# The next turn's rows turned later in the first expert turn, and the gate copies moved behind the first rows

## What is computed

```python
def swiglu(x, w_gate, w_up, w_down):
    return (jax.nn.silu(x @ w_gate) * (x @ w_up)) @ w_down

def moe_ffn(x, w_router, e_gate, e_up, e_down):
    logits = jnp.einsum('btd,de->bte', x, w_router, preferred_element_type=jnp.float32)
    top_v, top_i = lax.top_k(logits, TOP_K)
    w = jax.nn.softmax(top_v, axis=-1)
    gates = jnp.sum(jax.nn.one_hot(top_i, N_EXPERTS, dtype=jnp.float32) * w[..., None], axis=-2)
    out = jnp.zeros(x.shape, jnp.float32)
    for e in range(N_EXPERTS):
        out = out + gates[..., e:e + 1] * swiglu(x, e_gate[e], e_up[e], e_down[e]).astype(jnp.float32)
    return out.astype(x.dtype)
```

## Time and profile before

| | us |
|---|---|
| median of 3 runs (lowest, highest) | 1843.89 (1839.78, 1846.74) |
| the profiled execution | 1837.21 |
| its span, first to last instruction | 1835.4 |
| TensorE busy | 1629.8 |
| VectorE busy | 775.1 |
| ScalarE busy | 630.0 |
| GpSimd busy | 426.8 |

### The profile page before, as it was taken

How to read it: one execution, slowest core, us unless ns; L and a number is a source line. 1 busy time by engine, 2 the same in 40 slices (tenths; PEclk the granted TensorE clock), 3 DMA queues, 4 the chain that set the end, 5 groups by cost and what they waited for, 6 DMA issues and landing times.

```text
span 1835.4 us, 25783 instructions
## 1 busy us (share of the span) xinstructions
PE 1629.8 (89%) x10579; PEld 1447.5 (79%) x10580; DVE 775.1 (42%) x1073; ACT 630.0 (34%) x781; POOL 426.8 (23%) x209
## 2 busy tenths in 40 slices
PE   5999998979999999999699998988578998998991
PEld 2898667869999999998598766877577987897891
DVE  1204666351222222222512566533757545744742
ACT  3410443343111111112521244224356344644631
POOL 1430004344333333333442002430511010110003
PEclk9999999989999999999799998996689999998996
DMA  8220673214122211111031253101578564875834
GB/s 341 104 73 31 230 253 130 77 47 150 69 85 78 88 69 69 69 69 69 23 130 49 88 194 144 69 23 58 204 242 309 212 227 164 299 239 174 297 116 139
DMA packets 42285, 252.44 MB, mean 138 GB/s; under 512 B 5024, under 2 KB 7200, under 8 KB 15936
## 3 DMA queue, kind: packets, MB, share of 16 engines
q1 hardware_dynamic: 35200, 226.67, 34.2%
q0 software_dynamic: 6256, 21.56, 4.4%
q10 hardware_dynamic: 720, 2.62, 0.4%
HBM read 231.43 MB, written 19.46 MB: 137 GB/s over the span
## 4 chain that ended last, share of the span: by engine, by line
PE 74%; DVE 10%; DMA 5%; ACT 5%; issue 3%; POOL 3%; SPq 0%; POOLq 0%; DVEq 0%; ACTq 0%
PE ps L376 26%; PE ps L768 11%; PE ps L674 8%; PE ps L781 5%; PE ps L641 5%; DMA raw<-stream 4%; PE ps L481 3%; PE ps L502 2%; PE ps L586 2%; DVE wl L1807 2%; DVE smn L1528 2%; DVE probs L1544 2%; ACT wh L1359 2%; PE ps L513 1%; PE ps L572 1%
## 5 line engine op out<-in xcount | busy, mean ns | idle before, releaser
L993 POOL TENSOR_TENSOR wl<-raw,wh 128x2048 fp32r<-128x2048 f32 x61 | 286.7, 4709 | 743.6 <-ACT wh L1156 743.4
L768 PE MATMUL ps<-wh,xg 128*128 128x256 f32 x1536 | 295.4, 290 | 21.6 <-issue 15.9
L1807 DVE TENSOR_TENSOR wl<-raw,wh 128x2048 fp32r<-128x2048 f32 x96 | 219.9, 2292 | 136.9 <-ACT wh L1359 133.4
L768 PEld LDWEIGHTS ps<-wh,xg 128*128 128x128 f32 x1536 | 250.3, 198 | 24.9 <-issue 21.6
L376 PE MATMUL ps<-hn_h,wh 128*128 128x320 f32 x1088 | 252.2, 313 | 13.4 <-ACTq L1341 8.4
L376 PE MATMUL ps<-hn_l,wh 128*128 128x320 f32 x1088 | 249.2, 310 | 0.0
L376 PE MATMUL ps<-hn_h,wl 128*128 128x320 f32 x1088 | 249.1, 310 | 0.0
L1359 ACT CAST wh<-raw 128x2048 fp32r<-128x2048 f32 x96 | 183.1, 1909 | 124.8 <-PE ps L768 48.9
L768 PE MATMUL ps<-wl,xg 128*128 128x256 f32 x768 | 221.5, 288 | 0.0
L376 PEld LDWEIGHTS ps<-hn_h,wh 128*128 128x128 f32 x1088 | 182.6, 189 | 18.2 <-ACTq L1341 11.0
L376 PEld LDWEIGHTS ps<-hn_h,wl 128*128 128x128 f32 x1088 | 183.2, 189 | 0.0
(11 more groups left out here) (243 smaller groups left out, 2671.3 us busy)
## 6 DMA issues: line engine op xcount, KB each, us to landing
raw<-stream SPq DMA_DIRECT2D x205, 1024.0 KB, 4.8
sum_d<-zero POOLq DMA_DIRECT2D x7, 512.0 KB, 6.1
x<-x SPq DMA_DIRECT2D x5, 512.0 KB, 9.8
hn_d<-hrow ACTq DMA_DIRECT2D x5, 512.0 KB, 2.6
eacc<-sum_d SPq DMA_DIRECT2D x5, 512.0 KB, 5.9
y<-x SPq DMA_DIRECT2D x5, 512.0 KB, 2.6
hn_d<-zero POOLq DMA_DIRECT2D x2, 512.0 KB, 11.7
consts<-consts SPq DMA_DIRECT2D x1, 968.5 KB, 4.8
```

What stands on the lines that cost most here:

```text
L768: last = mm(bank(b, st * COLS, (st + 1) * COLS), xg[h][:, k, part, st * 128:(st + 1) * 128], w[:, k * COLS:(k + 1) * COLS], start=(k == 0 ...
L993: nc.gpsimd.tensor_tensor(wl[s][:, :], raw[s][:, :], wh[s][:, :].bitcast(F32), ALU.subtract).then_inc(wl_ready, 1)
L1807: v.tensor_tensor(wl[s][:, :], raw[s][:, :], wh[s][:, :].bitcast(F32), ALU.subtract).then_inc(wl_ready, 1)
```

## The change

In the first turn alone (`first_turn`: p + h == 0) TensorE turns tile 0 of the next turn's rows behind gate 3 in place of gate 2, with its wait for the gather, into bank 1; and tiles 1, 2 and 3 behind down 2, into banks 3, 1 and 3. ScalarE and VectorE take the tiles up in the order that answers to it. Ahead of the first turn VectorE copies the gate rows behind the first rows' low parts and subtraction 2. No operation is added or taken away.

```diff
--- before.py
+++ after.py
@@ -344,6 +344,9 @@
         slot_ready = sem("slot_ready")
         ADDED_0 = 16 * (NT + 2)
 
+        def first_turn(p, h):
+            return isinstance(p, int) and p + h == 0
+
         def named(p):
             return p if isinstance(p, int) else "more"
 
@@ -793,14 +796,20 @@
                                     pe.nop().then_inc(bank_full[6 + hf], 1)
                         if (kind, q) in (("gate", 1), ("gate", 2), ("gate", 3)):
                             turn_hidden(p, h, q - 1, tiles)
-                        if more and (kind, q) == ("gate", 2):
+
+                        late = first_turn(p, h)
+                        if more and (kind, q) == ("gate", 3 if late else 2):
                             pe.wait_ge(rows_here[1 - h], 32 + h * 32 + p * 32)
-                            turn_rows((named(p), h), 1 - h, 0, 3)
-                        if more and (kind, q) == ("gate", 3):
+                            turn_rows((named(p), h), 1 - h, 0, 1 if late else 3)
+                        if more and not late and (kind, q) == ("gate", 3):
                             turn_rows((named(p), h), 1 - h, 1, 1)
                         if (kind, q) == ("down", EXP_BLK - 2):
                             turn_hidden(p, h, EXP_BLK - 1, tiles)
-                            if more:
+                            if more and late:
+                                turn_rows((named(p), h), 1 - h, 1, 3)
+                                turn_rows((named(p), h), 1 - h, 2, 1)
+                                turn_rows((named(p), h), 1 - h, 3, 3)
+                            elif more:
                                 turn_rows((named(p), h), 1 - h, 2, 3)
                                 turn_rows((named(p), h), 1 - h, 3, 1)
 
@@ -1407,10 +1416,12 @@
                     if q < EXP_BLK - 1:
                         turned_by(act, (named(p), h, "exp", "gate", q + 1), p)
                         exp_split((5, 8, 11)[q], p, h)
-                    if q and nxt:
-                        rows_high((named(p), h), 1 - h, q - 1, p)
-                if nxt:
-                    rows_high((named(p), h), 1 - h, 3, p)
+                    late = int(first_turn(p, h))
+                    if q > late and nxt:
+                        rows_high((named(p), h), 1 - h, q - 1 - late, p)
+                for j in range(3 - late, 4):
+                    if nxt:
+                        rows_high((named(p), h), 1 - h, j, p)
                 if more:
                     exp_split(N_EU + 1, p, h)
                 if isinstance(p, int) and p + h == 0:
@@ -1835,7 +1846,8 @@
                 low(7, p, h)
                 hidden_low(1)
                 low(8, p, h)
-                if nxt:
+                late = int(first_turn(p, h))
+                if nxt and not late:
                     rows_low((named(p), h), 1 - h, 0, p)
                 product(2)
                 low(9, p, h)
@@ -1843,15 +1855,14 @@
                 hidden_low(2)
                 low(11, p, h)
                 if nxt:
-                    rows_low((named(p), h), 1 - h, 1, p)
+                    rows_low((named(p), h), 1 - h, 1 - late, p)
                 product(3)
                 if more:
                     low(N_EU, p, h)
                 hidden_low(3)
-                if nxt:
-                    rows_low((named(p), h), 1 - h, 2, p)
-                if nxt:
-                    rows_low((named(p), h), 1 - h, 3, p)
+                for j in range(2 - late, 4):
+                    if nxt:
+                        rows_low((named(p), h), 1 - h, j, p)
                 if more:
                     low(N_EU + 1, p, h)
                     low(N_EU + 2, p, h)
@@ -1861,10 +1872,10 @@
                 places()
                 low(0)
                 low(1)
-                gate_rows(3)
                 for j in range(4):
                     rows_low("ahead", 0, j)
                 low(2)
+                gate_rows(3)
                 for e in range(E):
                     expert_turn(e // 2, e % 2, e < E - 1, e < E - 1)
                 dve.wait_ge(trips_ready, 1)
```

## The result

The changed kernel takes 1837.13 us (median of 20 runs, 1831.12 to 1841.31), the kernel before 1843.15, measured beside it (median of 20). One of the 20 executions of before took 3240.27 us and is left out of the ratio; without it the median is 1842.68. The ratio is 0.997, 95% interval 0.9961 to 0.9979: 5.5 us faster, between 3.9 and 7.2. The profiled execution has a span of 1834.3 us.

A forecast was written before the change was run, and what follows sets the result against it. TensorE's work (89% busy) plus its holes was taken as the bound, here the 12.82 us wait for gathered rows. 8.6 gained less 2.4 for later rows gives 6.2 us: 1837.7 from the median 1843.89, range 1831.5 to 1844.5.

The forecast's parts named there:

- Three units ahead of the wait; the hole shrinks: TensorE, first turn: up, down and gate units run before the row wait; idle shrinks from 12.8 to 3.7 us.
- W: When the next turn's gathered rows land and TensorE's wait for them ends; 1337.03 in the profile before.
- The drag: GpSimd list writes meeting running VectorE weight subtractions wait for their end; the last write ends 3.2 us later.
- W moves by 1.0 or 3.7, 2.4 taken: Rows land later by 1.0 or 3.7 us, as the first gather slips through or is caught; middle 2.4.
- W + 17.8 to the next turn: First turn's work from W to the next turn's start takes 17.8 us against 26.41, a gain of 8.6.
- the wait for tile 3's bank: Tiles 1 and 3 share a bank: TensorE waits 0.84 for VectorE's subtraction, then 0.9 for transposes, until W + 11.5.
- the lower bound with the fast down: Last down of the first turn takes 2.75 in place of 4.49 us: W + 16.1, gain 10.3.
- Part 2: Gate copies behind the first rows: first product 2.9 us earlier, copies covered, worth nothing by themselves ahead of a wait.
- All behind moves as a whole: Everything behind the first turn is tied to it and moves as a whole; 6.2 us gained.
- No drag: Rival: GpSimd's chain keeps its times, W stays 1337.0, gain 8.6 to 10.3, 1834.5 us; chance 0.27.
- Eaten in the next turn: Rival: the next turn's weight waits lengthen, leaving a gain of 0 to 3, 1842.5 us; chance 0.17.
- The late landing: Rival: gathered rows land late beside three more weight units, W 1348.1, 2.4 us slower, 1846.3; chance 0.08.

The follow-up runs named there:

- The fillers: Kernel before plus, in idle VectorE time, a two-SBUF-input subtraction (last list write ends +22.49) or, in another kernel, a one-input reduction (+19.43); one execution each.
- e2: Kernel before with only the gate copies moved behind the first rows' low parts and third weight subtraction; 1843.28 us, ratio to before 1.0.
- e1: Changed kernel with the gate copies back at their old place, so only the next turn's rows are turned late; 1837.28 us, ratio to before 0.9965.
- e4: Kernel before with the first three weight subtractions moved into VectorE's idle time ahead of the list writes; 1835.0 us, ratio to before 0.9951.
- e7: Changed kernel with tile 3 turned behind the last down in place of ahead of it; ratio to before 0.9975.
- e3: Changed kernel with the first three weight subtractions moved into VectorE's idle time ahead of the list writes; 1834.3 us, ratio to before 0.9955.
- e9: Kernel before with tile 0 alone turned behind the second down unit in place of the third gate, first turn; 1835.93 us, ratio to before 0.9962.

## Why the prediction came out as it did

The forecast was 1837.7 and 6.2 us of gain; measured are 1837.13 and 5.5, or 6.0 by the medians with the 3240.27 in. The number is closer than the steps are, which partly cancelled. By its steps:

- *Three units ahead of the wait; the hole shrinks.* Right. The hole went to 7.64 us, which with the later W and the earlier start was the expected 5 to 9.
- *The drag.* Right, in mechanism and size: the last write at +22.88 against a forecast +22.63, with just the four writes caught that were named (five, eight, nine, ten). The fillers and the row subtractions leave the second SBUF input as the cause. The first gather slipped through, which had been too near to call. One reading was wrong: not seven but six of the ten writes of before were free (four took 1.88 to 3.06); it stood on the side of the rival.
- *W moves by 1.0 or 3.7, 2.4 taken.* By the profile 1.96, made up of 0.4 more than the forecast end of the second gather's writing and a landing 0.6 slower (6.85). As a term of the kernel's time the 2.4 is not shown: e2 costs nothing (1.0, 0.9989 to 1.001), and e1 against the changed kernel shows no gain that the intervals can tell from none. In W it shows only weakly. The four kernels whose writes end at 19.4 have W of 38.4 to 41.7, the four at 22.4 to 22.9 have 39.7 to 43.7, so the drag is real on GpSimd and W's own scatter is as large.
- *W + 17.8 to the next turn.* Measured 16.9, but not by the forecast's terms. The last hidden low part ended at W + 10.3 (forecast 9.8), the wait for tile 3's bank came as forecast, and the last down started at W + 11.7 (forecast 11.5). From the hidden low part on the forecast added the bank wait, a down of 4.49 and a branch of 1.83, together 8.0 us; measured are 6.55, and 6.4 to 6.8 in every kernel. So neither the bank wait (1.7) nor the down's clock has a price of its own, and the lower bound with the fast down is no case: e4, with a fast down and no bank wait, needed 6.55 too.
- *Part 2.* The first product comes 2.0 us earlier, not 2.9: +6.20 against +8.24, since the transposes ended 0.3 later than before and TensorE waited 1.11 us behind them and not 0.5. In the profiles of e7 and e2, with the same order, it came at +5.38 and +5.68, so this too scatters. That the copies are covered held; that the move is worth nothing in itself held too.
- *All behind moves as a whole.* In the profile the next turn's start gains 7.6 us where 6.2 were forecast, the first eviction 7.9 and the end 4.4. Whether the change gives any of it back one pair of executions can't tell. The one-tile turns (second, fifth, seventh) differ by several us from one execution to the next in every kernel, and the profile of before had the shortest of all. From first to last eviction it took 434.9 us, the changed kernel 437.9, the ten others 437.9 to 444.1. The many executions keep 5.5.
- *Rivals.* "No drag" fell by the list writes. "Eaten in the next turn" fell as stated, yet its ground lies near: in e1 and e3 waits for weights (10.4 and 10.3 us on ScalarE, 3.0 before) appear as soon as the rows are no longer late, in the first turn itself. The forecast stood because the hole, 7.64, was still wide in the changed kernel. The late landing didn't come.

What stays open: what fills the 6.4 to 6.8 us from the last hidden low part to the next turn, and why W differs by 3 us between executions with the same list writes. Its parts can be read from the traces: from the last write to the first gather 9.0 to 11.7 us (11.7 in e9, where GpSimd's cast of the table met a weight subtraction and took 2.26 in place of 0.22), from the first gather's start to the second's end 2.3 to 5.8 by which of them are caught, and the landing 5.4 to 7.5 (the eight kernels without early subtractions). What sets the landing was not separated. And the changed kernel and e1, e7 and e9 can't be ranked with these runs.

## What to carry over

When an engine's queue waits at one place for something that comes late, moving that place behind ready work wins, but only until the next supply sets the pace. Here waits for weights came up behind the rows: ScalarE's waits for raw grew from 3.0 to 10.4 us as the hole closed. Before moving the waiting place, look at what makes the awaited thing late: three subtractions put into idle time ended GpSimd's list writes 6 us earlier, and the kernels that have them took 1834.3 and 1835.0 us against the 1837.1 of the reordering. Before pricing a wait, look whether the next stage's start moves with it: tile 3's wait for its bank was real, and the next turn started 6.55 us behind the last hidden low part with it and 6.56 without. And compare such kernels by many runs or by marks from a common event in the trace; a single pair of spans would have said 1.1 us here.

## What the runs showed of the hardware

An indirect DMA's instruction on GpSimd (128 rows) takes 0.93 to 1.01 us alone (1.09 the first gather of a kernel), and when it starts while a VectorE subtraction with two SBUF inputs runs it ends 0.81 to 0.89 us behind that, 1.5 to 3.1 us in all. A reduction of 2.28 us with one SBUF input, and copies from PSUM, leave it alone. So does a subtraction that starts after it: a gather that began 0.2 us ahead of a subtraction took 1.01, and the subtraction its usual 2.29. One gather, in e9, began 0.04 us behind a subtraction's start and took 0.94; that subtraction took 2.37, the longest weight subtraction in the twelve traces' expert parts. And a write that stood behind one subtraction was not caught again by the next that followed without a gap: the first list write ended 0.9 us into the second of two subtractions in all kernels that have them there (2.28 us, and 1.01 in e3, which hasn't).

The page "SBUF — State Buffer" of the Trainium skill ("Who interferes with whom") states the rule: a VectorE instruction with two SBUF inputs contends with a GpSimd instruction that reads SBUF, one with at most one SBUF input, outside VectorE's 2-port modes, does not. The fillers agree with it, both ways. That the later one blocks in full, as the prediction has it, these traces show for GpSimd alone: where that gather began first, the later subtraction lasted 2.29 us like the others.
